# Two stacked transformer blocks on one core: the first block's steps in one table, attention of one stream placed among the tiles of the other

## The reference, cut to what matters

```python
# first block, two layers; x and ctx are [1, 256, 1024] f32
hx = modulate(rms_norm(x, g_norm1[l]), sh1_x, sc1_x)      # and hc from ctx
qa, ka, va, qb, kb, vb, qc, kc, vc = jnp.split(hx @ w_in[l], bounds, axis=-1)
# a: 8 query heads on 2 key heads, rope; b: neighbourhood window with a bias table
# c: 4 differential heads, w = softmax_0 - lam * softmax_1, rope, rms_norm of the result
# q and k of each head are rms-normed; x attends to [x, ctx], ctx to ctx alone
x = x + gt1_x * (jnp.concatenate([oa, ob, oc], axis=-1) @ w_out[l])
hx2 = modulate(rms_norm(x, g_norm2[l]), sh2_x, sc2_x)
x = x + gt2_x * conv_ffn(hx2, w_up[l], conv_w[l], conv_b[l], w_down[l])
# conv_ffn: u, g = split(dwconv3(h @ w_up)); (silu(g) * u) @ w_down
# ctx the same in layer 0; in layer 1 ctx only gives keys and values
```

## Time and profile before

| what | value |
|---|---|
| median of 3 runs | 2347.3 us (2344.55 to 2347.64) |
| profiled execution | 2349.55 us, span of its instructions 2347.8 us |
| TensorE busy | 2171.6 us, 92% |
| VectorE busy | 1538.6 us, 66% |
| ScalarE busy | 1222.5 us, 52% |
| GpSimd busy | 395.3 us, 17% |
| moved by DMA | 378.86 MB, mean 161 GB/s |
| mean granted TensorE clock | 0.960 |

### The profile page before, as it was taken

How to read it: one execution, slowest core, us unless ns; L and a number is a source line. 1 busy time by engine, 2 the same in 40 slices (tenths; PEclk the granted TensorE clock), 3 DMA queues, 4 the chain that set the end, 5 groups by cost and what they waited for, 6 DMA issues and landing times.

```text
span 2347.8 us, 41845 instructions
## 1 busy us (share of the span) xinstructions
PE 2171.6 (92%) x17176; PEld 1979.6 (84%) x17176; DVE 1538.6 (66%) x2387; ACT 1222.5 (52%) x2075; POOL 395.3 (17%) x483
## 2 busy tenths in 40 slices
PE   6998878999999999799998989998998999998998
PEld 3885547899999987479997879998997888998997
DVE  3555655777777756657776678856555668965555
ACT  3533755555555552665555665554444656564443
POOL 0020000233233202003330113211110103311110
PEclk8998979999999999899999999999998999998999
DMA  8534354465555543434653534554553444454552
GB/s 331 161 113 171 134 204 135 153 203 188 163 185 188 170 149 131 144 129 143 200 189 107 176 112 165 164 184 131 188 187 101 146 139 141 165 171 128 189 188 89
DMA packets 103197, 378.86 MB, mean 161 GB/s; under 512 B 11584, under 2 KB 11744, under 8 KB 101984
## 3 DMA queue, kind: packets, MB, share of 16 engines
q1 hardware_dynamic: 101520, 367.31, 47.3%
q10 hardware_dynamic: 1488, 8.89, 1.0%
HBM read 375.10 MB, written 1.05 MB: 160 GB/s over the span
## 4 chain that ended last, share of the span: by engine, by line
PE 35%; DVE 7%; issue 7%; ACT 3%; POOL 2%; DVEq 0%; POOLq 0%; ACTq 0%
PE ps L368 10%; PE ps L370 10%; PE ps L369 10%; DVE WL L1548 2%; PE ps L425 2%; DVE R L1558 2%; POOL R L2453 1%; ACT WH L926 1%; DVE RST L1584 1%; DVE TMP L1558 1%; PE ps L382 1%; PE ps L383 1%; POOL R L2412 1%; PE ps L388 0%; PE ps L805 0%
## 5 line engine op out<-in xcount | busy, mean ns | idle before, releaser
L368 PE MATMUL ps<-X,WH 128*128 128x256 f32 x4384 | 1243.2, 284 | 10.8 <-DVE WL L1548 9.9
L369 PE MATMUL ps<-X,WH 128*128 128x256 f32 x4384 | 1227.7, 280 | 0.0
L370 PE MATMUL ps<-X,WL 128*128 128x256 f32 x4384 | 1227.4, 280 | 0.0
L1548 DVE TENSOR_TENSOR WL<-RAW,WH 128x1024 fp32r<-128x1024 f32 (+2 forms) x608 | 802.8, 1339 | 474.6 <-ACT WH L926 474.2
L368 PEld LDWEIGHTS ps<-X,WH 128*128 128x128 f32 x4384 | 827.7, 189 | 30.6 <-DVE WL L1548 15.0
L369 PEld LDWEIGHTS ps<-X,WH 128*128 128x128 f32 x4384 | 827.5, 189 | 1.6
L370 PEld LDWEIGHTS ps<-X,WL 128*128 128x128 f32 x4384 | 827.1, 189 | 0.0
L926 ACT ACTIVATE WH<-RAW 128x1024 fp32r<-128x1024 f32 (+2 forms) x608 | 625.0, 1046 | 383.0 <-PE ps L370 365.9
L2351 POOL TENSOR_TENSOR TMP<-TMP 128x256 f32<-128x256 f32 x66 | 48.9, 741 | 741.5 <-ACT TMP L1260 738.0
L1558 DVE SCALAR_TENSOR_TENSOR TMP<-ps,PARS,TMP 128x255 f32<-128x255 f32 x264 | 124.1, 480 | 10.0 <-ACT TMP L1256 1.6
L575 PEld LDWEIGHTS ps<-PTB,R 128*64 128x64 f32 x768 | 48.8, 148 | 90.6 <-DVE PTB L1738 43.8
(11 more groups left out here) (183 smaller groups left out, 2126.0 us busy)
## 6 DMA issues: line engine op xcount, KB each, us to landing
RAW<-w_dram SPq DMA_DIRECT2D x674, 512.0 KB, 3.9
RAW<-w_dram SPq DMA_DIRECT2D x16, 480.0 KB, 3.3
BIG<-big_dram ACTq DMA_DIRECT2D x4, 1024.0 KB, 6.1
RAW<-w_dram SPq DMA_DIRECT2D x8, 320.0 KB, 2.7
RAW<-w_dram SPq DMA_DIRECT2D x6, 384.0 KB, 3.1
XT<-x_dram ACTq DMA_DIRECT2D x2, 1024.0 KB, 10.9
CONS<-con_dram ACTq DMA_DIRECT2D x1, 1774.0 KB, 8.1
out_dram<-XT SPq DMA_DIRECT2D x1, 1024.0 KB, 3.9
```

Source lines behind the costliest of these rows:

```text
L368: e.matmul(out, a.hi, b.hi, start=start and i == 0, stop=False, skip_group_check=open_bank)
L369: e.matmul(out, a.hi, b.lo, start=False, stop=False, skip_group_check=open_bank)
L370: last = e.matmul(out, a.lo, b.hi, start=False, stop=stop and i == n - 1, skip_group_check=open_bank)
L1548: e.tensor_tensor(weights(i).lo, raw(i), weights(i).hi.bitcast(F32), ALU.subtract).then_inc(*w_lo.mark(i))
```

## The change

The orders of the first block are replaced by one list, STEPS, built at import by `first_block`, and every engine (and the packing of weights) walks it. The first block is put in this order: ada steps; statistics of both streams; the norm and the projection of ctx, with the norm of x between; the projection of x with the attention of ctx and 16 ada steps between its tiles; out product of ctx; norm and feed-forward of ctx with the attention of x between its tiles; out product of x; norm with 8 ada steps; feed-forward of x. In layer 1 the two projections are cut in parts and the attention of x lies between the later parts.

- q and k are normed in four groups of two to four tiles: sums of the tiles of a group go to rows 32 j of one bank by matmuls in different 32-column groups, root and reciprocal (VectorE) are done per group, the spreads read different 32-row groups.
- `two_tiles` is no longer used in the first block. The norm per chunk is scale, high, low in turn.
- Scaling of the exponentials by the reciprocal goes from ScalarE (L1071) to GpSimd, 128 x 512 or 128 x 256, two per unit. Reciprocals of a unit are one VectorE instruction.
- The gate is silu(g) u = (g/2)(1 + tanh(g/2)) u, the halves folded into the convolution's weights (two small VectorE operations per layer): tanh on ScalarE, and on GpSimd two products, a sum, the high and the low part, five operations and not three.
- Transposes and values use the PS ring too, and q, k tiles the LONG ring. The value result is copied per unit of 128 columns. Buffers are placed anew; the gate's activations have seven buffers of their own.
- The gain and lambda steps of layer 0 stand ahead of the first norm, those of layer 1 ahead of the last feed-forward of layer 0.
- The constants loaded are fewer (2019 columns, not 3805). The second block is otherwise unchanged.

```diff
+GROUPS = [["ka", "qa0", "qa1"], ["qa2", "qa3"], ["kc0", "kc1", "qc0", "qc1"], ["kb0", "kb1", "qb0", "qb1"]]
+UNITS = [(t, qt) for t in (0, 1, 2, 3, 6, 7, 4, 5) for qt in range(2)]
...
+def weave(main, *sides):
+
+    out = [list(s) for s in main]
+    for side, a, b in sides:
+        for n, s in enumerate(side):
+            out[a + n * (b - a) // len(side)] += s
+    return out
...
+    steps = ada * 4 + [[("stat", 1)]] + ada * 4 + [[("turn_ada",)], [("stat", 0)], [("gains", 0)]] + norm_slots(("n1", 0, 1))
+    steps += weave(project_slots(0, 1, [[0, 1], 0, [2], 1, [3]]), (norm_slots(("n1", 0, 0)), 1, 17))
+    x = project_slots(0, 0, [[0, 1], 0, [2], 1, [3]])
+    steps += weave(x, (attend_slots(0, 1, list(range(16))), 2, len(x)), (ada * 16, 0, len(x)), ([[("mask", 0)]], 6, 7)) + [[("turn_ada",)]]
+    steps += out_slots(0, 1) + [[("rstd", ("out", 0, 1))]]
+    main = [[] for _ in range(10)] + ffn_slots(0, 1)
+    steps += weave(main, (norm_slots(("n2", 0, 1)), 0, 10), (attend_slots(0, 0, list(range(16))), 0, len(main)))
...
+                elif kind == "qsum":
...
+                    for j, name in enumerate(members(l, st, g)):
...
+                        last = e.matmul(bank.ap[32 * j:32 * j + 32, 0:256], halves_of(name)[0], k.square[l, st, name].ap, start=True, stop=True)
...
+                        rows, bank = slice(32 * j, 32 * j + 32), PS.take()
...
+                        e.matmul(bank.ap[:, 0:256], halves_of(name)[1][rows], r.ap[rows], start=True, stop=True).then_inc(*spread.mark(("qk", l, st), name))
...
+                    e.activation(b.ap, act["g"].ap, ACT.Tanh, scale=0.5).then_inc(*gated.mark(tag, j))
...
+                    for s in range(2):
+                        n = 8 + (2 * s if tile_ > 5 else s)
+                        e.tensor_scalar(p[s].ap[:, 0:nk], p[s].ap[:, 0:nk], b.ap[:, n:n + 1], None, ALU.mult).then_inc(*weighed.mark(tag, u, s))
...
+                    e.tensor_tensor(u, u, g, ALU.mult).then_inc(*pooled.mark(tag, j, 0))
...
+                    e.tensor_tensor(b.ap, b.ap, u, ALU.mult).then_inc(*pooled.mark(tag, j, 1))
...
+                    e.tensor_tensor(b.ap, b.ap, u, ALU.add).then_inc(*pooled.mark(tag, j, 2))
...
+                    e.tensor_copy(a.ap.hi, b.ap).then_inc(*gate_hi.mark(tag, j))
...
+                    e.tensor_tensor(a.ap.lo, b.ap, a.ap.hi.bitcast(F32), ALU.subtract).then_inc(*gate_lo.mark(tag, j))
```

## The result

The changed kernel takes 2500.3 us (median of 4 runs, 2498.08 to 2504.03), the kernel before on the same chip 2347.5 (4 runs): a ratio of 1.065, 95% interval 1.0626 to 1.0673. That is 153 us slower, where 55 us faster was forecast, and 208 us over the forecast time.

The account below looks back on a forecast made before the run. TensorE, busy 92% of the span, was taken as the bound, with losses mainly in attention latency chains. First-block stages summed to 1201 us against 1256, 55 less: 2349.5 - 55 - 2 = 2292 us, range 2238 to 2348.

Parts of the forecast that it names:

- (C): Layer 0, projection of x with the context's attention and 16 ada steps: 122 us, 15 of them waits.
- (F): Layer 0, feed-forward of the context with thirteen attention units of x: 254 us, 27 of them waits.
- (L): Layer 1, rest of both projections with x's attention and 12 ada steps: 137 us, 18 of them waits.
- Low-clock stretches mostly gone between 113 and 235 us: Sign for the forecast, in (C): TensorE's stretches at low clock would mostly disappear there.
- (H): Layer 0, norm and eight ada steps ahead of the feed-forward of x: 17 us, bound by VectorE's 19 us.
- (N): Layer 1, norm between the out product and the last feed-forward of the first block: 12 us.
- (E): Layer 0, norm after the context's out product, with only three attention units beneath: 23 us.
- the regrouping's gain: First block, q and k norms: 15 grouped sets at 0.5 us replace 88 serial matmuls, 23 us less.
- Rival 1: Better cover: waits in (C), (F), (L) fall from 60 to some 15 us, clock stays granted; 2247 us, chance 0.22.
- Rival 2: Half the cover fails: shared four-bank PSUM ring, serial spreads, 12 units at 2 us more; 2328 us, chance 0.14.
- The wait for a bank in front of up tiles: Sign against the forecast: waits in front of up tiles for a PSUM bank; no size given.
- Rival 3: GpSimd slows VectorE, which bounds all woven stages; splits of 1.6 us or more show it; 2370 us, chance 0.13.

Follow-up runs that it names:

- r12: r9 with the attention of the context unwoven from the projection of x, on its own PSUM banks: ratio 1.0149.
- r6: Changed kernel with its table in plain order (attentions unwoven), transposes and values on their own PSUM banks: ratio 1.0444.
- r7: r6 with scaling on ScalarE, values ahead of transposes and the silu gate: ratio 1.0105.
- r9: Changed kernel, still woven, with scaling on ScalarE, values ahead of transposes and the silu gate: ratio 1.0302.
- r13: r7 with the ada steps moved from the norms of x and of layer 1 into attentions: ratio 1.0106.
- r14: r13 with the stages in the order of the kernel before: ratio 1.0003.
- r18: Kernel before with scaling on GpSimd and values behind transposes: ratio 1.0154.
- r15: r14 with the statistic of x, gains and lambda moved to the beginning of the context's projection: ratio 0.9999.
- r4: Changed kernel with the silu gate as before, three GpSimd instructions instead of five: ratio 1.0567.

## Why the prediction was wrong

**The sum of what was found.** From 153 us over the kernel before: 82 for scaling, order of values and gate together; 36 for the weave of (C) with its shared banks; 10 for the other two weaves with theirs; 0 for moving ada steps out of the norms; 24 for the order of the stages; 1 left. Each is a difference between two kernels that ran, and holds for this order of undoing them. The 82 are not a cost of the weave: in plain order with own banks the same three parts are 79. Weave and banks can't be told apart in the woven stages, since tiles of v and down products need the banks there; in plain order, with the chain unmended, banks alone were 15 us.

**The step that failed is the cover in (C), (F) and (L).** I counted TensorE's own work between scores and transposes (5 us, later 9, in (C)) and set against it the bare latency of the chain, 3.2 us, or 5 to 6 "with the splits queued". The reciprocal in the timeline above is eleven microseconds behind the exponentials. What I called cover on TensorE comes with work on VectorE, ScalarE and GpSimd that stands ahead of the chain in queues kept in order, and part of it waits for TensorE or for a transfer itself. For my waits of 15, 27 and 18 us TensorE is idle 56, 32 and 42 us, and in (C) its busy time is 49 us over my sum, 24 of which remain when the weave is undone (r12). The upper bounds that I gave, 35, 50 and 40, came from adding up latencies, not from following one unit through all five queues, and were passed in (C) and, by 2 us, in (L). Nor was the lack of cover the weave's alone: with the attentions unwoven, on own banks, the chain in its new form (scaling on GpSimd, values behind the transposes) costs 73 us (r6 to r7). I had given that form no term beside those waits.

**The clock was left out of the price.** "Low-clock stretches mostly gone between 113 and 235 us" was the reverse of what came: 0.79 in (C), lower than in either attention of layer 0 in the kernel before, 0.89 and 0.82. Where products were woven into waiting work, the lower clock fell on the products too (0.85 over all 192 us of r9's stage); unwoven it fell on the attention alone (0.97 and 0.80 in r12's two stages).

**The order of values and transposes was in the difference and got no term.** The two stand the other way round than before. In the kernel before that is worth 8 us, in the changed kernel 67, when it is undone alone. I took the gain of the table from its slots and didn't compare what stands directly ahead of the waiting transposes.

**(H) and (N)**: the norms exposed are 30 and 22 us, for 17 and 12. I took VectorE's work as the bound and gave the ada steps beside it no term; without them the gap is 10 us where it was 34 (r13). The 24 us that r14 gave back come from putting the norms of (E) and (H) beneath other work again, with the old order of the stages; (N) stays exposed in it.

**GpSimd's scaling** was 1.57 us for 512 columns, for my 1.2 between 0.94 and 1.49. The error is 0.37 us, twice a unit in 32 units: 24 us of its time at most, a small part of 186. That GpSimd's queue of five gate instructions would matter held: 27 us of waits for the scaling were forecast in (F), 14.3 appear, and the silu gate gives 19 us back, 16 of them in (F).

**What held**: the projection of the context (61 us forecast, 63 measured), both feed-forwards of x (192 and 188 forecast, 195 and 197 measured), the second block, and roughly the grouped sums and spreads: TensorE is busy 0.6 to 0.9 us with a set, for 0.5, and waits 7 us in all for the reciprocals ahead of the spreads. In r7 there are 130 us from the first projection matmul (55.8) to the first score (185.5), in the kernel before 152 (43.6 to 195.4), with four ada steps among them, 5 us; that includes the regrouping's gain that I had priced at 23 us over the whole block.

**The rivals.** Rival 1 (better cover) is excluded by the idle times above. Rival 2 (half of the cover fails, 2328 us) had part of the mechanism: shared banks, 15 us in r6, and in r12 together with the weave. Its price, 36 us over the forecast, was a sixth of the 208. The wait for a bank in front of up tiles that I had named as a sign against me is there, though small (L502 behind ScalarE's exponential, 6.5 us in two places of (F)). Rival 3 (VectorE slowed by GpSimd) gave the right sign for the wrong reason. The splits in (F), min/median/max, in the changed kernel:

```profile
L1653 DVE TENSOR_TENSOR WL<-RAW,WH x65: 1152/1226/1776, 379.1 to 668.0; 128x1024 fp32r<-128x1024 f32 x65
```

The median is 1.23 us, where I had set 1.5 and rival 3 needed 1.6, although GpSimd is busy 139 of 292 us there; before it was 1.44 with GpSimd busy a third. In the feed-forward of x after, with GpSimd busy 111 of 195 us, the median is 1.35. VectorE's share of the span fell to 62%. The Trainium skill, "SBUF — State Buffer", section "Who interferes with whom", lets a VectorE instruction with two SBUF inputs wait for one of GpSimd that reads SBUF; the longest split, 1.78 us, may be such a case, but the load of GpSimd did not say how often the two meet. The Trainium skill, "Perfetto Trace Analysis", section "Matmul Optimizations", asks that all eight PSUM banks be used; r6's 15 us agree with it in direction, for the attentions in plain order. In the woven stages the other four banks are in use too, by tiles and down products.

**What stays open.** How the 36 us of (C) divide between shared banks and steps queued ahead of the chain; a woven stage with own banks, or one whose splits are issued behind the reciprocals, was not tried. Why the two parts of r18 cost 36 us in the kernel before and 73 in r6 is open too. Where r15 gives back what it gains can be read: at the residual sum behind layer 0 it is 17 us ahead of the kernel before (804.1 for 820.8 us), at the first score of layer 1 11 (916.3 for 927.1), and behind that attention, which holds four ada steps more, it is 3 us late (1041.4 for 1038.5). Why that attention is longer by more than those steps, 5 us, was not tried. No version ran faster than the kernel before; r15 at 0.9999 is level.

## What to carry to other kernels

Work woven between two steps of a chain is cover only on the engine that waits; on each other engine of the chain it is a queue ahead of it, so before weaving follow one unit through every queue, write down what stands directly ahead of each of its steps, and whether that waits itself. Keep matmuls that run at full clock apart from stretches in which TensorE waits. Where two changes touch the same wait, undo them one by one and together: here 68, 67 and 19 us alone were 82 together. And measure a part in the kernel that it is meant for: the two parts that cost 36 us in the kernel before cost twice that in the new table.

## What the runs showed of the hardware that I had not expected

GpSimd's multiplication of a tile by a per-partition scalar takes 929 ns for 128x256 and 1570 ns for 128x512 here, 1.9 and 2.2 times ScalarE's 502 and 717 ns. 28 more table loads of 1283 ns on ScalarE, all in one stage, were cheaper than 44 more GpSimd instructions in it, of 0.75 and 1.18 us, in the queue ahead of scalings (r4). A weight split's median fell from 1.44 to 1.23 us where GpSimd's busy share rose from a third to 48%, and was 1.35 at 57%. TensorE's granted clock was 0.79 over a stage of 212 us in which it was busy 74% of the time.
